# First MLP product of a transformer layer, weights stationary instead of tokens

## What is computed

```
u = rms_norm(h, norm_mix_g)
h = h + nsa_mixer(u, nsa_w_in, ..., nsa_w_out)
u = rms_norm(h, norm_mlp_g)
h = h + square(relu(u @ mlp_w1)) @ mlp_w2          # 2048 -> 8192 -> 2048
gate = sigmoid(rms_norm(h, ple_norm_g) @ ple_w_gate)
h = h + gate * (p @ ple_w_proj)
```

## Time and profile before

| | |
|---|---|
| median of three runs | 1246.81 us (1245.11 to 1247.39) |
| the profiled execution | 1245.18 us, its span 1243.4 us |
| TensorE matmuls busy | 1231.9 us, 99% |
| weight loads busy (beside the matmuls) | 1019.5 us, 82% |
| vector engine / scalar engine busy | 700.1 us, 56% / 571.4 us, 46% |
| DMA | 222 MB, 179 GB/s over the span |

### The profile page before, as it was taken

One profiled execution on the slowest core, in us unless ns is written; L12 is line 12 of the kernel. 1 busy time (PEld: TensorE's weight loads), 2 busy tenths in 40 slices (PEclk: granted clock), 3 DMA queues, 4 the chain that ended last, 5 costly groups with the idle time before them and its releaser, 6 DMA issues.

```text
span 1243.4 us, 16016 instructions
## 1 busy us (share of the span) xinstructions
PE 1231.9 (99%) x5838; PEld 1019.5 (82%) x5838; DVE 700.1 (56%) x965; ACT 571.4 (46%) x783; POOL 57.5 (5%) x57
## 2 busy tenths in 40 slices
PE   8999999999999999999999999999999999999998
PEld 6888788888888888888888888788888888888886
DVE  4676646887766644545445455454545445555654
ACT  6554343555445544443344443444433445445543
POOL 0000000000000001000010000000000001000000
PEclk9999999999999999999999999999999999999999
DMA  9666754333335565556665556665556665555551
GB/s 320 204 202 203 200 170 147 107 118 102 102 119 186 174 198 174 196 190 195 195 173 193 191 189 196 182 183 189 189 195 191 185 191 182 185 193 176 200 194 64
DMA packets 123726, 222.07 MB, mean 179 GB/s; under 512 B 8981, under 2 KB 18569, under 8 KB 123657
## 3 DMA queue, kind: packets, MB, share of 16 engines
q1 hardware_dynamic: 123656, 221.07, 56.2%
HBM read 218.95 MB, written 2.10 MB: 178 GB/s over the span
## 4 chain that ended last, share of the span: by engine, by line
PE 96%; DVE 2%; DMA 1%; POOL 1%; ACT 0%; issue 0%; SPq 0%; ACTq 0%
PE acc L1089 86%; PE tr L1142 2%; PE sc L1209 1%; DMA w_raw<-in_nsa_w_in_dram 1%; POOL rs L391 1%; PE sc L1222 1%; DVE w_lo L708 1%; PE sc L1208 1%; PE tr L1131 0%; PE sc L1131 0%; PE acc L1116 0%; PE tr L1260 0%; PE tr L1256 0%; PE tr L1257 0%; PE tr L1237 0%; PE tr L1241 0%
## 5 line engine op out<-in xcount | busy, mean ns | idle before, releaser
L708 DVE TENSOR_TENSOR w_lo<-w_raw,w_hi 128x1024 fp32r<-128x1024 f32 (+1 forms) x413 | 509.1, 1239 | 442.9 <-ACT w_hi L434 439.9
L434 ACT ACTIVATE w_hi<-w_raw 128x1024 fp32r<-128x1024 f32 (+1 forms) x413 | 435.2, 1059 | 439.8 <-PE acc L1089 431.4
L1089 PE MATMUL acc<-w_hi,a_hi 128*128 128x512 f32 x960 | 384.0, 400 | 3.9 <-DVE w_lo L708 2.4
L1089 PE MATMUL acc<-w_hi,a_lo 128*128 128x512 f32 x960 | 374.3, 390 | 0.0
L1089 PE MATMUL acc<-w_lo,a_hi 128*128 128x512 f32 x960 | 373.8, 389 | 0.0
L1089 PE MATMUL acc<-w_hi,b_hi 128*128 128x512 f32 x640 | 254.5, 398 | 0.0
L1089 PE MATMUL acc<-w_hi,b_lo 128*128 128x512 f32 x640 | 249.4, 390 | 0.0
L1089 PE MATMUL acc<-w_lo,b_hi 128*128 128x512 f32 x640 | 249.1, 389 | 0.0
L1089 PEld LDWEIGHTS acc<-w_hi,a_hi 128*128 128x128 f32 x960 | 180.4, 188 | 44.4 <-issue 5.7
L1089 PEld LDWEIGHTS acc<-w_lo,a_hi 128*128 128x128 f32 x960 | 180.5, 188 | 37.9 <-issue 2.4
L1089 PEld LDWEIGHTS acc<-w_hi,a_lo 128*128 128x128 f32 x960 | 180.2, 188 | 38.1
(11 more groups left out here) (161 smaller groups left out, 605.7 us busy)
## 6 DMA issues: line engine op xcount, KB each, us to landing
w_raw<-in_mlp_w_dram SPq DMA_DIRECT2D x256, 512.0 KB, 3.7
w_raw<-in_nsa_w_in_dram SPq DMA_DIRECT2D x80, 512.0 KB, 4.1
w_raw<-in_nsa_w_out_dram SPq DMA_DIRECT2D x32, 512.0 KB, 3.8
w_raw<-in_ple_w_gate_dram SPq DMA_DIRECT2D x32, 512.0 KB, 4.1
w_raw<-in_nsa_cmp_w_dram SPq DMA_DIRECT2D x8, 512.0 KB, 5.0
w_raw<-in_ple_w_proj_dram SPq DMA_DIRECT2D x4, 512.0 KB, 4.1
out_dram<-h SPq DMA_DIRECT2D x7, 256.0 KB, 4.5
h<-in_x_dram SPq DMA_DIRECT2D x3, 512.0 KB, 8.5
```

The costliest lines, as they stand in the source:

```text
L434: nc.scalar.activation(w_hi[:, u % SPLIT, 0:width], w_raw[:, u % RAW, 0:width], ACT.Copy).then_inc(hi_done, 1)
L708: nc.vector.tensor_tensor(w_lo[:, u % SPLIT, 0:width], w_raw[:, u % RAW, 0:width], f32(w_hi[:, u % SPLIT, 0:width]), ALU.subtract).then_in ...
L1089: last = nc.tensor.matmul(acc[c % 2][t][:], xs[:, kt, toks], ws[:, u % SPLIT, m * NW:(m + 1) * NW], start=(kt == 0 and n == 0), stop=(kt = ...
```

## The change

In the first MLP product the roles are exchanged: 128 columns of the weights are stationary and all 256 tokens move. A hidden chunk is now four result tiles of 128 hidden columns by 256 tokens, each in half of its own bank. The result comes out transposed, with hidden columns on the partitions, as the second product wants it. So:

- a unit of a hidden chunk is 24 matmuls of 256 columns (`hidden_unit`), each behind its own LDWEIGHTS of 128 columns, where 12 of 512 columns were; the second product is as before (`down_unit`).
- the 8 transposes of each of the 16 hidden chunks are gone, and GpSimd's squares with them.
- the scale of a token must now lie along the free dimension, the same on all partitions: in the first MLP chunk the vector engine spreads it (`spread`), TensorE turns it in 2 transposes at unit 7, and the vector engine copies it to rstd_row.
- the vector engine reads the four banks (ReLU and scale in one instruction each, at k == 2), the scalar engine squares (k == 2) and copies to b_hi (k == 3), the vector engine subtracts to b_lo (k == 4).
- hidden and down chunks share all eight banks (`hidden_banks`, `down_banks`); one semaphore, chunk_read, counts the chunks read, and a chunk waits for the read of the one two before it.
- pt_hi and pt_lo move from the end of the memory to behind b_lo, and an unused tensor of 384 bytes a partition (lead_in) stands ahead of all.

```diff
-        pt_hi = sb("pt_hi", [P, 2, SEQ], F32R)
-        pt_lo = sb("pt_lo", [P, 2, SEQ], F32R)
+        sb("lead_in", [P, 96])
         h = sb("h", [P, TT, D])
...
         b_lo = sb("b_lo", [P, KT, SEQ], F32R)
+        pt_hi = sb("pt_hi", [P, 2, SEQ], F32R)
+        pt_lo = sb("pt_lo", [P, 2, SEQ], F32R)
...
+        rstd_row = q_t[:, 0]
...
+        def hidden_banks(j):
+
+            return [tr[0], tr[1], *acc[0]] if j % 2 else [sc[0], sc[1], *acc[1]]
+
+        def down_banks(j, last):
+
+            return (acc[1], sc, acc[0], acc[1])[j - 4] if last else (sc, acc[1], tr, acc[0])[j - 4]
+
+        def gate_read(n):
+
+            return 6 - n % 2 + n // 2
...
-            def square(c, i=0):
-                for t in range(TT):
-                    pool.wait_ge(acc_read[c % 2][t], c // 2 + 1 + 4 * i)
-                    nc.gpsimd.tensor_tensor(stage[:, t], stage[:, t], stage[:, t], ALU.mult)\
-                      .then_inc(squared, 1)
-
-            with pool.Fori(0, QUARTERS) as q:
-                for j in range(4):
-                    square(C_MLP + j, q)
...
-                    for k in split_hi(FIRST[C_MLP + j], UPC, i):
+                    c = C_MLP + j - 1
+                    for k in split_hi(FIRST[c + 1], UPC, i):
                         if k == 2:
-                            evac(C_MLP + j - 1, lambda t: stage[:, t], ACT.Relu, rstd[:, 1], i)
-                        if k == 4:
-                            transposed_hi(R_MLP + j - 1, b_hi, 4 * (j - 1), None, i)
+                            act.wait_ge(chunk_read, 4 + j + 8 * i)
+                            for b in range(2):
+                                nc.scalar.activation(stage[:, b], stage[:, b], ACT.Square).then_inc(squared, 1)
+                        if k == 3:
+                            for b in range(2):
+                                act.wait_ge(squared, 2 * (j - 1) + b + 1 + 8 * i)
+                                nc.scalar.activation(flat(b_hi, 4 * (j - 1) + 2 * b, 2), stage[:, b], ACT.Copy)\
+                                  .then_inc(hidden_hi, 1)
...
+                if k == 5:
+                    dve.wait_ge(rs_ready, 9)
+                    nc.vector.tensor_copy(junk[:, 0:SEQ].rearrange("p (t s) -> p t s", t=TT),
+                                          rstd[:, 1, :, None].to_broadcast([P, TT, P])).then_inc(spread, 1)
+            dve.wait_ge(spread_full, 1)
+            nc.vector.tensor_copy(rstd_row, tr[0][:, 0:SEQ]).then_inc(rstd_row_ready, 1)
+            dve.wait_ge(rstd_row_ready, 1)
...
+                        if k == 2:
+                            dve.wait_ge(unit_used, END[c] + 8 * UPC * i)
+                            for m, bank in enumerate(hidden_banks(j - 1)):
+                                ins = nc.vector.scalar_tensor_tensor(
+                                    out=stage[:, m // 2, m % 2 * SEQ:(m % 2 + 1) * SEQ], in0=bank[:, 0:SEQ],
+                                    scalar=0.0, in1=rstd_row, op0=ALU.max, op1=ALU.mult)
+                            ins.then_inc(chunk_read, 1)
                         if k == 4:
-                            transposed_lo(R_MLP + j - 1, b_hi, b_lo, 4 * (j - 1), None, i)
+                            for b in range(2):
+                                kt = 4 * (j - 1) + 2 * b
+                                dve.wait_ge(hidden_hi, 2 * (j - 1) + b + 1 + 8 * i)
+                                nc.vector.tensor_tensor(flat(b_lo, kt, 2), stage[:, b], f32(flat(b_hi, kt, 2)),
+                                                        ALU.subtract).then_inc(hidden_split, 1)
...
+            def hidden_unit(j, k, i=0):
+
+                u = FIRST[C_MLP + j] + k
+                if k == 0:
+                    pe.wait_ge(chunk_read, j + 3 + 8 * i)
+                pe.wait_ge(lo_done, u + 1 + 8 * UPC * i)
+                for kt in range(UNIT_KT * k, UNIT_KT * (k + 1)):
+                    for m, bank in enumerate(hidden_banks(j)):
+                        at = (kt % UNIT_KT) * NW + m * P
+                        for n, (ws, xs) in enumerate(((w_hi, a_hi), (w_lo, a_hi), (w_hi, a_lo))):
+                            last = nc.tensor.matmul(bank[:, 0:SEQ], ws[:, u % SPLIT, at:at + P], xs[:, kt],
+                                                    start=(kt == 0 and n == 0), stop=(kt == KT - 1 and n == 2))
+                last.then_inc(unit_used, 1)
+
+            def down_unit(j, k, i, last_q=False):
+
+                u = FIRST[C_MLP + j] + k
+                if k == 0:
+                    pe.wait_ge(chunk_read, j + 3 + 8 * i)
+                if j == 4:
+                    pe.wait_ge(hidden_split, k + 1 + 8 * i)
+                pe.wait_ge(lo_done, u + 1 + 8 * UPC * i)
+                for kt in range(UNIT_KT * k, UNIT_KT * (k + 1)):
+                    for t in range(TT):
+                        last = tile_product(down_banks(j, last_q)[t], u, kt, t, b_hi, b_lo)
+                last.then_inc(unit_used, 1)
+
+            def ple_gate_unit(n, k):
...
+                if k == 7:
+                    pe.wait_ge(spread, 1)
+                    for t in range(TT):
+                        last = nc.tensor.transpose(tr[0][:, t * P:(t + 1) * P], junk[:, t * P:(t + 1) * P], ident[:])
+                    last.then_inc(spread_full, 1)
                 split_by(R_H1, k)
-                unit(C_MLP, FIRST[C_MLP] + k, k, a_hi, a_lo)
-
-            def hidden_chunks(i):
-
-
-                for j in range(1, 5):
+                hidden_unit(0, k)
+            pe.wait_ge(rstd_row_ready, 1)
+
+            with pe.Fori(0, QUARTERS - 1) as q:
+                for j in range(1, 4):
                     for k in range(UPC):
-                        if k == 2:
-                            pe.wait_ge(squared, TT * j + 4 * TT * i)
-                            transpose_set(R_MLP + j - 1, from_stage, i)
-                        if j == 4:
-                            split_by(R_MLP, k, i)
-                        x_hi, x_lo = (b_hi, b_lo) if j == 4 else (a_hi, a_lo)
-                        unit(C_MLP + j, FIRST[C_MLP + j] + k, k, x_hi, x_lo, i)
-
-            with pe.Fori(0, QUARTERS - 1) as q:
-                hidden_chunks(q)
-                for j in range(5, 9):
-                    x_hi, x_lo = (b_hi, b_lo) if j < 8 else (a_hi, a_lo)
+                        hidden_unit(j, k, q)
+                for j in range(4, 8):
                     for k in range(UPC):
-                        unit(C_MLP + j, FIRST[C_MLP + j] + k, k, x_hi, x_lo, q)
+                        down_unit(j, k, q)
+                for k in range(UPC):
+                    hidden_unit(8, k, q)
             last_q = QUARTERS - 1
-            hidden_chunks(last_q)
-            for n in range(3):
-                c = C_MLP + 8 * last_q + 5 + n
+            for j in range(1, 4):
                 for k in range(UPC):
-                    if k == 2:
-                        staged(c - 1)
-                        transpose_set(R_H2 + n, from_h(n))
-                    unit(c, FIRST[c] + k, k, b_hi, b_lo)
+                    hidden_unit(j, k, last_q)
+            for j in range(4, 8):
+                for k in range(UPC):
+                    if j > 4 and k == 2:
+                        pe.wait_ge(chunk_read, 4 + 8 * last_q + j)
+                        transpose_set(R_H2 + j - 5, from_h(j - 5))
+                    down_unit(j, k, last_q, True)
```

More of the change, by code:

```diff
@@ L119 @@
 R_H1 = p_set(H - 1) + 1
[L120 to L121 removed]
+R_H2 = R_H1 + 4
 def hi_sets(r):
@@ L254, in trunk_layer @@
         o_done = sem("o_done")
+        chunk_read = sem("chunk_read")
+        spread = sem("spread")
+        spread_full = sem("spread_full")
+        rstd_row_ready = sem("rstd_row_ready")
         squared = sem("squared")
+        hidden_hi = sem("hidden_hi")
+        hidden_split = sem("hidden_split")
         tile_complete = sem("tile_complete")
@@ L468, in sum_squares, with h_chunk_stats @@
                         link(ins)
-            def h_chunk_stats(c, norm, n):
-                for t in range(TT):
-                    act.wait_ge(acc_read[c % 2][t], c // 2 + 1)
+            def h_chunk_stats(count, norm, n):
+                act.wait_ge(chunk_read, count)
                 sum_squares(norm, n)
@@ L882, in head_o, with add_to_h @@
                   .then_inc(o_done, 1)
-            def add_to_h(c, n, i=0):
+            def add_to_h(c, n, banks, i=0):
                 dve.wait_ge(unit_used, END[c] + 8 * UPC * i)
@@ L887, in add_to_h @@
                     cols = h[:, t, n * NW:(n + 1) * NW]
-                    nc.vector.tensor_tensor(cols, acc[c % 2][t][:], cols, ALU.add).then_inc(acc_read[c % 2][t], 1)
+                    ins = nc.vector.tensor_tensor(cols, banks[t][:], cols, ALU.add)
+                ins.then_inc(chunk_read, 1)
             def constants(n, at, cols):
@@ L1059, in gated_out @@
             def gated_out(n, t, at=0, cols=NW, part=0):
-                c = C_PLE + n
-                dve.wait_ge(acc_read[c % 2][t], c // 2 + 1 + part)
```

(47 more changed lines are left out.)

44 lines of the change are left out of this document (18 added, 26 removed).

## The result

The changed kernel takes 1257.12 us (median of four, 1256.01 to 1258.50) against 1245.96 us for the kernel before in the same comparison: ratio 1.0097, 95% interval 1.0085 to 1.0109. It is slower by about 11 us; 1241.5 was forecast. The profiled execution took 1256.39 us, its span is 1254.5.

What follows compares the result with a forecast made beforehand. TensorE was taken as the bound, busy for 99% of the span. 1245.2 - 13.9 (transposes) + 4.8 (matmuls) + 3.9 (back edges) + 0.2 - 0.3 = 1239.9, plus 1.6 for the median: 1241.5 us, range 1232 to 1257.

Steps and rivals of the forecast that it cites:

- The matmul's price: Hidden chunks: 1536 matmuls of 512 columns become 3072 of 256 at 115 ns each, +4.8 us.
- the rub: Load and stream of nearly equal length cost 1 to 5 ns over either; 1.5 ns was added to 113.5.
- The second rival (B): Hidden matmuls: the excess over full rate follows columns loaded; 120.3 ns for 256 columns, 1257.8 us; chance 0.19.
- The argument I held against it: A 512-column matmul beside a load of 48 should take about 220 ns, but the trace has 0.23 us.
- The back edge: TensorE's loop branch: cover counted as 17.5 queued matmuls falls from 3.96 to 2.0 us, +3.9 us in two edges.
- no term below is about the clock: Whole span: the granted clock is full, 2.4 GHz, so no forecast term was given to it.
- The transposes: Hidden result: 8 transposes in each of 16 chunks, 0.87 us per set, leave TensorE's chain, -13.9 us.
- the two scale transposes: First MLP chunk: two transposes turn the token scales into a row, +0.2 us.
- the place of pt: Matmuls on pt_hi and pt_lo, moved next to b_lo, go from 232.5 to 226.9 ns each, -0.3 us.
- all four waits: MLP: waits for w_lo at unit 3, the scale spread, the banks and the first down product stay hidden, 0 us.
- A: The forecast case: loads hide behind streaming, 113.4 to 116 ns a matmul, 1232.7 to 1244.6 us; chance 0.58.
- the chance of 0.61: Whole kernel: the chance given to a faster result, under 1244.3 us.

Runs made afterwards that it cites:

- e5: Changed kernel with fewer columns streamed, one width per chunk, behind 128 stationary columns; 1154.28 us in one run, work left out, so only paces are read.
- e1: Kernel before with each 512-column matmul of the 16 hidden chunks issued as two of 256, transposes kept; 1271.99 us, ratio 1.0211.
- e6: Changed kernel with fewer stationary columns loaded (96, 64 or 32), one number per chunk; 1179.50 us in one run, work left out.
- e2: Changed kernel with w_hi loaded once for both activation halves: one 512-column and one 256-column matmul replace three of 256; 1243.45 us, ratio 0.9985.
- e3: Changed kernel with TensorE's loop over the first three quarters written out three times; 1249.40 us, ratio 1.0033 to the kernel before.

## Why the prediction was wrong

**The matmul's price, the step that failed.** "Streaming costs about 0.443 ns a column at either width, and I see no reason for less" led to 115 ns and +4.8 us; it measured 120.0 ns and +20.1 us. Two rows that fit one line, 226.9 at 512 and 113.8 at 256, had different loads behind them (128 and 48 columns), and I read the line as a price for each column. With the load kept at 128 the price is for each matmul (e5), and it was doubled in number. That term is 15.3 us, where 15.6 lie between 1241.5 and 1257.1. That the two are so near is in part chance, since other terms were off as well and nearly cancel: the edges cost more than was forecast (below), and the kernel before had a median of 1245.96 in the comparison, not the 1246.81 that the sum carried over. Another step was weak too: the nearest rows for the pair, taken for load and stream together, are plain fp32 matmuls (112.5 and 109 ns). They show 2 to 6 ns over their stream (some 107 ns by the estimate in the forecast), the fp32r pair 13.3 over its own, so the rub could not be carried from one format to the other; why they differ no run shows.

**The second rival (B).** Its 120.3 ns and 23.1 us a chunk were right, and e1 shows that the pair as such has this price. Its rule, that the excess follows the columns loaded, was right only in part (e6). The argument I held against it (a 512-column matmul beside a smaller load should be faster) therefore proved nothing: with 64 loaded the 512-column matmul is slower. It should have had more than 0.19, since it was the only reading in which the rows with 48, 63 and 128 columns all fitted.

**The back edge.** Right in kind, too small in size: the cover is a count of queued matmuls, 3.96 us with 512 columns, 2.0 now (626.9 to 628.9) and 3.06 with e2's mixture, some 17 matmuls each time, and e3 removes the stall. Forecast were +3.9 us in two edges. The traces have +2.9 (2.7 and 2.1 against 0.5 and 1.4) and +7.2 (4.0 and 4.0 against 0.3 and 0.5); by the medians, writing the loop out gave 7.7 us after and nothing before. What I left out is the clock: "no term below is about the clock" held for the trace before, but the longer stall brings the lower clock in some executions.

**What was right.** The transposes (-13.9 by rows, 14.9 between e1 and the changed kernel), the two scale transposes and the place of pt (0.2 and 0.3 us), and all four waits at 0: TensorE stands only at the two edges in the MLP, and e3's quarters leave no room for another wait. The sign of A, the low end of the range and the chance of 0.61 all hung on the one price.

## What to carry to other kernels

Price a matmul from two rows with the same format, the same load and different widths, before halving its width; a line through rows with different loads can hide a price that is paid for each instruction. Where an operation's count doubles, look first for what is paid per operation. When the matmuls ahead of a loop's branch become shorter, the branch comes out of its cover: write the loop out (e3), or put the wide ones there (e2's wider ones lost less at the edges; it was not tried by itself).

## What was not expected of the hardware

- A stall of 2.0 to 2.9 us on TensorE was followed at 7 of 14 edges by a stretch at a granted clock of 0.50, which cost 1.4 to 1.6 us more; behind stalls of 1.4 us or less it was not. The start of the program shows the same (0.43 us between 512-column matmuls where it is 0.23).
- Behind 512 streamed columns a load of 64 or 96 costs more (230 ns) than one of 128 (226.7); behind 256, one of 32 costs more (118) than one of 64 (113.7).
- Alternating matmuls of 512 and 256 columns take 353.2 ns a pair, in groups of eight 349 to 350, where runs of one width would add up to 346.7.
- The bracket behind a matmul names the last semaphore event, and at the back edge it named the vector engine, which had nothing to do with it.
